# Moving the weight buffers of an fp32 decoder kernel to other places modulo 128 bytes

## The reference, cut to what matters

```python
hn  = rmsnorm(x, w_pre_mix)
z   = hn @ w_in                       # q, k, v, gates of two head groups
...                                   # gated linear recurrence, sliding-window attention
mix = concatenate([o_g, o_s]) @ w_out
h   = x + rmsnorm(mix, w_post_mix)
f   = rmsnorm(h, w_pre_ffn)
f   = (silu(f @ w_gate) * (f @ w_up)) @ w_down
h   = h + rmsnorm(f, w_post_ffn)
h   = h + sigmoid(h @ w_ple_gate) * (p @ w_ple_proj)
```

## Time and profile before

| what | before |
|---|---|
| median of 3 runs | 2744.64 us (2744.17 to 2746.19) |
| span of the profiled execution | 2743.8 us |
| TensorE matmuls busy | 2681.6 us (98%) |
| TensorE weight loads busy | 2245.5 us (82%) |
| VectorE busy | 1233.3 us (45%) |
| ScalarE busy | 853.4 us (31%) |
| mean granted TensorE clock | 0.995 |

### The profile page before, as it was taken

How to read it: one execution, slowest core, us unless ns; L and a number is a source line. 1 busy time by engine, 2 the same in 40 slices (tenths; PEclk the granted TensorE clock), 3 DMA queues, 4 the chain that set the end, 5 groups by cost and what they waited for, 6 DMA issues and landing times.

```text
span 2743.8 us, 38814 instructions
## 1 busy us (share of the span) xinstructions
PE 2681.6 (98%) x15360; PEld 2245.5 (82%) x15360; DVE 1233.3 (45%) x2155; ACT 853.4 (31%) x1692; POOL 196.6 (7%) x384
## 2 busy tenths in 40 slices
PE   6999999999999999999999999999999999999998
PEld 4777777877787779987777787777787989999998
DVE  5455552655565673134432666344224561111234
ACT  4345532443434443122222343333122431000012
POOL 0032000111000000101110001121000000000000
PEclk9999999999999999999999999999999999999999
DMA  7865577877777696654444576444445575444453
GB/s 256 313 223 183 206 292 244 271 249 246 244 241 265 231 344 203 227 180 171 172 159 174 204 267 235 156 156 172 158 163 186 214 272 185 161 162 169 167 191 142
DMA packets 214308, 579.83 MB, mean 211 GB/s; under 512 B 25824, under 2 KB 64608, under 8 KB 213728
## 3 DMA queue, kind: packets, MB, share of 16 engines
q1 hardware_dynamic: 213488, 575.26, 59.8%
q0 software_dynamic: 640, 2.10, 0.2%
HBM read 430.80 MB, written 147.65 MB: 211 GB/s over the span
## 4 chain that ended last, share of the span: by engine, by line
PE 89%; DVE 5%; ACT 2%; DMA 2%; issue 1%; SPq 1%; POOL 0%; DVEq 0%; ACTq 0%; POOLq 0%
PE ps L2006 59%; PE ps L1923 20%; PE ps L2091 2%; PE ps L2111 1%; PE ps L2173 1%; PE ps L2211 1%; PE ps L2195 1%; PE ps L2200 1%; DMA wld<-wl 1%; DMA wh<-whd 1%; PE ps L2039 1%; DVE ssq L1574 1%; DVE wl L1522 0%; ACT wh L1142 0%; DVE mixF L1605 0%
## 5 line engine op out<-in xcount | busy, mean ns | idle before, releaser
L2006 PE MATMUL ps<-bh,wh 128*128 128x288 f32 (+1 forms) x1696 | 513.7, 346 | 1.8 <-ACT ta L1178 1.3
L2006 PE MATMUL ps<-bl,wh 128*128 128x288 f32 (+1 forms) x1696 | 508.7, 343 | 0.0
L2006 PE MATMUL ps<-bh,wl 128*128 128x288 f32 (+1 forms) x1696 | 508.6, 343 | 0.0
L2006 PEld LDWEIGHTS ps<-bh,wh 128*128 128x128 f32 x1696 | 295.5, 189 | 42.1 <-issue 6.3
L2006 PEld LDWEIGHTS ps<-bh,wl 128*128 128x128 f32 x1696 | 295.7, 189 | 35.8
L2006 PEld LDWEIGHTS ps<-bl,wh 128*128 128x128 f32 x1696 | 295.8, 189 | 33.5
L2006 PE MATMUL ps<-gh,wh 128*128 128x512 f32 (+1 forms) x880 | 289.7, 362 | 9.7 <-issue 4.8
L2006 PE MATMUL ps<-gl,wh 128*128 128x512 f32 (+1 forms) x880 | 284.8, 356 | 0.0
L2006 PE MATMUL ps<-gh,wl 128*128 128x512 f32 (+1 forms) x880 | 284.7, 356 | 0.0
L1536 DVE SCALAR_TENSOR_TENSOR tb<-ta,ps 128x512 f32<-128x512 f32 (+1 forms) x88 | 61.9, 704 | 388.8 <-ACT ta L1161 388.8
L1546 DVE TENSOR_TENSOR mixF<-mixF,ps 128x512 f32<-128x512 f32 (+1 forms) x160 | 112.1, 703 | 240.5 <-PE ps L2006 240.3
(11 more groups left out here) (212 smaller groups left out, 3897.2 us busy)
## 6 DMA issues: line engine op xcount, KB each, us to landing
wh<-whd SPq DMA_DIRECT2D x306, 512.0 KB, 3.7
wl<-wld SPq DMA_DIRECT2D x306, 512.0 KB, 4.6
w_raw<-in_w SPq DMA_DIRECT2D x102, 512.0 KB, 5.0
whd<-wh SPq DMA_DIRECT2D x102, 512.0 KB, 5.5
wld<-wl SPq DMA_DIRECT2D x102, 512.0 KB, 6.3
zt<-zd SPq DMA_DIRECT2D x16, 1024.0 KB, 7.7
zd<-zst SPq DMA_DIRECT2D x56, 256.0 KB, 5.0
res_m<-in_x SPq DMA_DIRECT2D x24, 256.0 KB, 6.3
```

Of the source, the lines that this page charges most:

```text
L2006: last = MM(out, ww[SLOT[n]][:, w_], xx[:, kk, r_], start=(j == 0 and x == 0), stop=(j == len(ks) - 1 and x == 2))
```

## The change

The tensors of slots 0 and 1 are replaced by two larger ones with slices in them, and small unused tensors are put ahead of five places so that these begin at a chosen number of bytes modulo 128. Slot 0 (high and low) then begins at 48, slot 1 at 96, slot 2 stays at 32. The sums of squares (sq, ssq_part, ssq) move from 96 to 32 with S, kw, vsp and kdec behind them; mean_r and head_r stay at 32; w_lr and gate_up go from 0 to 96; ta stays at 96; mixF goes from 32 to 96; the arena, and with it every moving operand of a unit, stays at 32. No instruction is added, removed or put in another order.

```diff
+LINE, PHASE = 128, 32
...
-        wh = [sb(f"wh{s}", [P, KM * P], f32r) for s in range(2)]
-        wl = [sb(f"wl{s}", [P, KM * P], f32r) for s in range(2)]
+        def pad_to(name, phase=PHASE):
+
+            n = (phase + (-nc.sbuf_base // 32) * 32) % LINE
+            if n:
+                sb(name, [P, n // 4])
+
+
+        pad_to("before_first")
+        first = sb("w_first", [P, 2 * KM * P + 8], f32r)
+        pad_to("before_second", PHASE + 64)
+        second = sb("w_second", [P, 2 * KM * P], f32r)
+        wh = [first[:, 4:4 + KM * P], second[:, 0:KM * P]]
+        wl = [first[:, 4 + KM * P:4 + 2 * KM * P], second[:, KM * P:2 * KM * P]]
...
+        pad_to("before_means")
         mean_at = -(-nc.sbuf_base // 32) * 32
...
+        pad_to("before_squares")
         sq_at = -(-nc.sbuf_base // 32) * 32
...
-        base = nc.sbuf_base
+        pad_to("before_arena")
+        base = -(-nc.sbuf_base // 32) * 32
```

## The result

The changed kernel takes **2729.36 us** (median of four runs, 2726.99 to 2730.25), against 2745.41 us of the kernel before, run beside it (four runs, 2744.17 to 2747.85). The ratio is 0.9936, with a 95% interval of 0.9924 to 0.9948: 16 us less, where 39 were forecast.

The account below looks back on a forecast made before the run. The bound was the pace at which TensorE starts matmuls, set by where weights lie. From 2744.64 us, 39 us came off for units in slots 0 and 1, all other terms 0: 2705 us, 8-in-10 range 2655 to 2765.

Parts of the forecast that it names:

- the step that took 226.7 for places 48 and 96: 512-column matmuls of slots 0 and 1, chunks 0 to 2: pace falls from 234.3 to 226.7 ns.
- the term of 39 us: 242 units of chunks 0 to 2 in slots 0 and 1, each falling by 0.16 us from 5.62 to 5.46.
- Chunk 3 at nothing: Units of chunk 3, 288 columns: stay at 133.3 ns, cost 0, bounds 22 us either way.
- The other matmuls at nothing: Scores, values and states at new places: 0 for all together, with 3 us either way.
- Loads to a place of 16 bytes at nothing: Slot 0's loads and stores, rows beginning at 48: cost 0, a landing twice as long still covered.
- the writers hidden: ScalarE and VectorE writing the slots, 1055 and 1228 ns per unit in 5.6 us of matmuls: cost 0.
- The head means must stay: Sign in the changed profile: head-mean matmuls, weights and moving operand both at 32, stay at 226.7 ns.
- Only the equal place helps: Rival for slots 0 and 1: places 48 and 96 go on at 234 ns; 2744 us, chance 0.13.
- One slot gains, the other stays: Rival: only one of slots 0 and 1 quickens, half of 39 us; 2725 us, chance 0.12.
- The new places collide more: Rival: slots 0 and 1 slow to 240.0 ns, 33 us, 2778; one slot 16 us, 2761; chance 0.18.
- A lower step: Rival: 512-column matmuls settle at 220.0 ns, 82 us less, 2662; with chunk 3 at 126.7, 2640; chance 0.09.
- Slow transfers: Rival: slot 0's transfers at a 16-byte place take twice the time, 43 us; 2748 to 2788, chance 0.04.

Follow-up runs that it names:

- the kernel with distance 0: Against the changed kernel: pads by 256, slots 0 and 1 at 32 modulo 256 like the moving operands; 2716.4 us, ratio 0.9896.
- the kernel with slot 1 at distance 0: Against the changed kernel: pads by 256, slot 0 kept at 176 (distance 144), slot 1 moved to 32 modulo 256; 2721.55 us, ratio 0.9911.

## Why the prediction was right or wrong

**Right: what bounds the kernel, and the way the change acts.** TensorE's pace depends on where operands lie, and the gain is in that pace: its busy time fell 17.6 us with nothing else moved, and the experiment that moved most other tensors and kept the distance gave ratio 1.0. (The unit that the prediction reads as slot 1 is slot 0, as the names in the changed kernel's timeline show; both lay at one place, so nothing hangs on it.) The size of a settled stream was right as well: 39 us were worked out for two slots that settle, and with both at distance 0 the undisturbed steps (under 0.30 us) from one 512-column unit matmul to the next fell by 38.7 us (their sum went from 1619.3 to 1575.8 us; 21 fewer of them, at 0.23 us, are 4.8 of that).

**Wrong: the step that took 226.7 for places 48 and 96.** The prediction put 48 beside the earlier trace rows because it is 16 bytes from 32, and took 96 with it as the less certain half. Three things failed there.
- *Modulo 128.* It read the head mean as proof that only the place modulo 128 counts. That row has weights and moving operand at the same place modulo 256 as well, so it could not tell the two apart. By 256 the distances are 144 and 192, not 16 and 64, and neither is near 0.
- *The nearest row.* Even by the right modulus nearness is a poor guide: 226.7 settled at 0, 227.7 at 240, 229.2 at 16, but 233.1 at 32 already, and 229.3 again at 192.
- *One pace for one place.* At 144 there are two. In chunk 0's ffn stage, where no slot-2 unit leads in, slot 0 goes at 232.5 ns, against 234.2 before and 227.4 with distance 0; the stage takes 430.5, 435.7 and 425.7 us.

So the term of 39 us was mis-sized. In the changed kernel the same undisturbed steps fell by 28.8 us, 27 of them fewer: at 0.23 us these are 6.2, which leaves **22.6 us** from the pace.

**Missing from the sum: what is given back.** 22.6 us of pace became 16. The steps of 0.30 us and longer between two such matmuls, where a wait, a unit's start or a lower clock breaks the stream, went from 247 to 274 and from 117.9 to 130.5 us; less the 6.2 that those 27 would have taken anyway, 6.4 us went back there. (Chunk 3's unit matmuls took 2.0 us less and all other stretches 2.9 us more; together that is the 15.4 us of the span, within rounding.)

Most of the 6.4 is the granted clock. At the lower of its two levels, 1.2 GHz, the step is 427 ns. Steps of 0.40 to 0.50 us, most of them 427 ns, were 55 in the trace of before (23.8 us) and 85 in that of the changed kernel (36.7 us): 12.9 us more, of which 30 ordinary steps of 0.233 us would be 7.0. That leaves 5.9 us for the clock. Here is one wait for weights, in the changed kernel and then in the kernel before (start us, us, line, operands, idle time ahead and its releaser; then busy time by stretch, with the granted clock third from the end):

```profile
462.63 3.45 PE L1939 MATMUL ps<-dh,w_second 128*128 128x512 f32 x8 [2.81 <-DMA w_second<-whd]
463.00:466.40 3.40, 3.40 (x10) 2.65 (x9) 0.00 (x0) 0.00 (x0) 0.00 (x0) 0.51 1.00 316
```
```profile
463.73 2.14 PE L1923 MATMUL ps<-dh,wh 128*128 128x512 f32 x8 [2.60 <-DMA wh<-whd]
464.10:467.50 3.40, 3.40 (x16) 2.75 (x15) 0.00 (x0) 0.00 (x0) 0.00 (x0) 1.00 0.91 278
```

After an idle time of 2.81 us the clock fell to half, and eight matmuls took 3.45 us; after one of 2.60 us it stayed up, and they took 2.14. That the quicker pace brings such falls is not shown: the kernel with distance 96 and the rest moved has 83 of these steps at the old pace, and over the fourteen traces they run from 54 to 85. The sum had no term for them. In the four executions of the changed kernel the mean granted clock was 0.992 to 0.993, against 0.995 in the profiled execution of before and 0.993 to 0.996 in those run beside the experiments.

With distance 0, 38.7 became 29. There the steps of 0.40 to 0.50 us are only a few more (64), but the waits grew: the rows of who waited for whom on TensorE add up to 55.4 us before, 57.5 in the changed kernel and 60.3 with distance 0. Those rows that matter (us in total, times, longest us), the changed kernel:

```profile
PE ps L1939 <- DMA w_second<-whd: 4.6, 2, 2.8
...
PE ps L2022 <- issue: 3.9, 4, 2.2
PE ps L1939 <- ACT w_second L1158: 3.6, 1, 3.6
...
PE ps L1939 <- ACT w_first L1158: 2.5, 2, 1.6
PE ps L1939 <- DMA w_first<-whd: 2.1, 1, 2.1
```

the kernel with distance 0:

```profile
PE ps L2023 <- issue: 6.7, 5, 3.0
PE ps L1940 <- ACT w_slot L1159: 6.6, 4, 3.8
...
PE ps L1940 <- DMA w_slot<-whd: 5.6, 3, 2.0
```

and the row of the kernel before that stands beside those of the earlier trace rows:

```profile
PE ps L2006 <- issue: 4.8, 3, 2.7
```

The waits for loads of high weights went from 5.6 to 6.7 (4.6 and 2.1) in the changed kernel and stayed at 5.6 with distance 0; those for ScalarE went from 5.6 to 6.1 and 6.6, those with no releaser in the profile (issue) from 4.8 to 3.9 and 6.7. A quicker TensorE comes earlier to places where it needs something that is no quicker than before; that this is why the waits grow with distance 0 is argued, no run took it apart.

**The other terms.** Chunk 3 at nothing: 132.8 against 133.3 ns, 2.0 us, near enough. The other matmuls at nothing: no gain in the run with ratio 1.0, and the 2.9 us more outside the unit matmuls lie within the 3 us allowed. Loads to a place of 16 bytes at nothing, and the writers hidden: right, 3.7 and 4.6 us to land, writers of 1053 to 1056 ns on ScalarE and 1227 to 1228 on VectorE as in the earlier trace rows. "Slot 2 must stay": right, 227.9 ns on average in both. "The head means must stay": wrong, and that was the sign of the wrong modulus.

**The rivals.** *Only the equal place helps* named the right thing, sameness of place, but by its price (2744) it fell: unequal places have paces of their own. *One slot gains, the other stays*, 2725, came nearest to the time, and that is luck: both gained in part, slot 1 5.0 ns a step and slot 0 3.3. *The new places collide more* fell: no distance of the sixteen is above 234.2 ns. *A lower step* fell: no run showed a settled step of 512 columns under 226.7. *Slow transfers* fell with the landings. The rule of the Trainium skill that was weighed ("TensorE: Matmul & The Clock Gate", Part 2, two independent read ports) gave no change. The runs disagree with what it would mean here: 226.7 to 234.2 ns for the same matmul by place alone. The 216 ns that the prediction set beside it the Trainium skill gives, in "Back-to-back issue gap" on the same page, for a single matmul's gap and without a word on places; for a stream of loads and matmuls it has some 131 ns, and no stream of 512 columns here settled under 226.7. The measurement decides.

## What to carry to other kernels

Where matmul follows matmul with new weights each time, look at the distance between the place of the weights and that of the moving operand modulo 256 bytes, and make it 0: here that is 29 to 30 us of 2745, and the least edit does as well as any version found, a pad of 96 bytes ahead of the arena and nothing else (2715.44 us, ratio 0.9887). Read it from step to step in the timeline, since durations of 396 and 394 ns hide it. And before a pace is carried from one row to a new place, ask which other rules would fit the same row: here a second modulus did.

## What the runs showed of the hardware that was not expected

- The pace of a stream of 512-column matmuls with a weight load for each has a memory of how it started: at distance 144 the same operands at the same places run at 226.7 or at 233.3 ns, each mostly kept through whole units until other matmuls or a pause come between. After such a break nearly all go on at 232.8 ns or more (51 of 52 in the kernel with slot 1 at distance 0).
- The streams that don't settle repeat patterns: 232, 232, 232, 237 ns at distance 144 when slow, 226, 229, 232 at 192, and steps from 228 to 241 at 128. What makes the pattern no run shows.
- 288 columns show little of it: 132.1 to 133.5 ns a step in nearly all runs and slots. In chunk 3 a unit's matmuls go by turns to the two halves of the tokens, which begin 1,152 bytes apart, so each distance comes by turns with the one 128 bytes from it; that 288 columns as such don't feel the distance is not shown. The lowest is slot 2 at 130.6 ns, steps of 129 and 131 by turns, in the run with slots 0 and 1 at 176 and 208; that stays unexplained.
- Waits of TensorE of nearly the same length were followed by either level of the granted clock: 2.81 us by the lower, 2.60 us at the same place in the kernel before by the higher. The kernel before and the one with the distance of before have the same pace and 55 and 83 steps of 0.40 to 0.50 us.
- Rows that begin at a multiple of 16 but not of 32 bytes are loaded and written as fast as others (loads land after 3.7 and 4.6 us; the writers take 1053 and 1227 ns, for rows at 96 1056 and 1228).
